# Hybrid decoder layer with a PEER expert stage: one weight half kept on chip, one projection half moved, twelve row buffers in place of six

## The chip, the cores and the metric
The kernel runs on 1 core of a Trainium2 chip. The metric is the device time in microseconds (us) of one execution; lower is better. A core has TensorE (PE, matmul; its weight loads are listed as PEld), VectorE (DVE), ScalarE (ACT), GpSimd (POOL) and SyncE (SP), and 16 DMA engines that serve all of its queues. Here SP issues the loads of weights (queue q1 in the profile) and POOL issues gathers of expert rows (queue q0).

## The reference
One layer on x (256 tokens x 1024, float32), with a memory of 256 tokens:
- RMSNorm, one projection `h @ w_in` to 3072 + 8 columns, 8 MoBA heads of 64 with a relative bias, 8 forgetting-attention heads of 64, an RMSNorm of either half, then `x += o @ w_out` (1024 x 1024).
- Cross-attention to the memory, 4 heads of 256, with `w_xq`, `w_xk`, `w_xv`, `w_xo` (1024 x 1024 each): `x += ...`.
- PEER: `h = RMSNorm(x)`, a routing query `h @ w_peer_query` (1024 x 1024, 8 heads of 2 x 64), scores against 2 x 128 sub-keys per head, the best 16 of either side, the best 16 of their 256 sums, and for each token and head 16 experts out of 16384:

```
u  = expert_down[eidx];  a = gelu(einsum('cd,chkd->chk', xc, u))
vv = expert_up[eidx];    y = einsum('chk,chkd->cd', g * a, vv)
```

`g` is the softmax of the 16 top scores. So each token reads 8 x 16 = 128 rows of `expert_down` and as many of `expert_up`. The output is a final RMSNorm. All in float32.

## The kernel before
**Tiles.** The 256 tokens are two tiles (t = 0, 1) of 128 tokens, one token per partition. `expert_down` and `expert_up` lie side by side in one table, so a gather of one slot brings 128 rows of 2048 floats, 1.05 MB: the first half of a row is for the dot product, the second is what is summed up. There are 2 x 128 slots n = 0 to 255 (`SPT` = 128 in a tile).

**Steps of a slot n.** POOL issues the gather into a row buffer (L554). DVE takes the dot product of the row's first half with the token (`dot`, L1017). ACT computes gelu, multiplies by the gate and writes a diagonal matrix of the result (`weight`, L722, L726, L729). PE multiplies that diagonal with the row's second half and accumulates (`up`, L1311: two products of 512 columns, which the profile lists as 4 MATMULs) and then increments `up_used`. There are `NS` = 6 row buffers: gather n waits until `up_used` says that slot n - 6 is done. Four of them are in `QKVB`, two in `SPARE`. `dots`, `gelu`, `wgt` and `diag` have 6 places as well.

**Order of the work.** Every engine runs a list of steps, written out by hand, in order (`main`, L120 to L176). It holds everything of tile 0 up to its routing query and all of tile 1's self-attention. Then come the slots. What tile 1 still needs (cross-attention, its routing query, its scores) and the second half of tile 0's routing query is put between tile 0's slots by the list `slots` (L179 to L189): PE does a step right after `up` of the slot named there, a step with four numbers in four quarters, and ACT and DVE do their part of it 4 slots later (`LAG`). The choice of experts for head H + 1 is spread over the slots of head H on DVE (`TOP`).

**Steps that the change touches.** `wout(t, i)` is output half i (512 columns) of `o @ w_out` of tile t, 8 products of 512 columns on PE; `wq(t, i)` is half i of the routing query, four heads, each 8 products of 128 columns; `sc` are the scores; `xq`, `xS`, `xPT`, `xO`, `xo` are cross-attention. In front of the slots the order is: a quarter of `wout(1, 1)`, the first routing head (`wq_first`) and its `top` (the choice of experts of head 0), the other three quarters of `wout(1, 1)`, `wq(0, 0)`, `sc(0, 0)`, `sc(0, 1)`, all of `wout(1, 0)`, then slot 0.

**Weights.** Weight halves of 2.1 MB are loaded by SP, in a fixed order, into six slots of the tile `weights` (`SLOT`, L73); `load_block` (L460) first waits until the last product that reads what lay there has been done (`used_up`). `w_peer_query`'s first half is loaded twice: early into `SPARE` for tile 0 (`wq_early`, L516), and again into weight slot 0, where `w_out`'s first half lay, for tile 1. Its second half goes into weight slot 1, where `w_out`'s second half lay, and serves both tiles. So SP's order here is: wait for `wout(1, 1)`, load half 1; wait for `wout(1, 0)`, load half 0; wait for `xo(1, 0)`, load the final gain. Since `SPARE` holds `wq_early`, gather 4 waits for `wq(0, 0)` (L551).

Of the kernel before, what the change touches and what calls it, by code (L numbers as in the profile page):

```python
# [60 lines left out]
def hybrid_layer(nc, A, out, bias_scratch):  # L61
# [96 lines left out]
    for part in range(4):  # L158
# [15 lines left out]
    main += rest[1][:1] + [("square_p", 0, 0), ("pT", 0, 1), ("start", 0, 0), ("wq_first", 0, 0), ("y_start", 0, 0),  # L174
                           ("sc_first", 0, 0), ("sc_first", 0, 1), ("root_p", 0, 0), ("top", 0, 0), ("y_start", 0, 1)]
    main += rest[1][1:] + [("wq", 0, 0), ("sc", 0, 0), ("sc", 0, 1)] + rest[0]  # L176


    slots = [((0, 1, 3, 4), ("wq", 0, 1)), (8, ("sc", 0, 2)), (9, ("sc", 0, 3)),  # L179
             (11, ("xT", 1, 0)), (11, ("xT", 1, 1)), (13, ("root_x", 1, 0)), (16, ("rstd_x", 1, 0)),  # L180
             ((19, 21, 23, 25), ("xq", 1, 0)), ((27, 29, 31, 33), ("xq", 1, 1))]
    for h in range(XH_N):
        slots += [(37 + 5 * h, ("xS", 1, h)), (42 + 5 * h, ("xnorm", 1, h)), (44 + 5 * h, ("xPT", 1, h)),
                  (49 + 5 * h, ("xO", 1, h))]
    slots += [((69, 71, 73, 75), ("xo", 1, 0)), ((77, 79, 81, 83), ("xo", 1, 1)), (85, ("xg", 1, 0)),
              (88, ("xg", 1, 1)), (89, ("square_p", 1, 0)), (90, ("pT", 1, 0)), (90, ("pT", 1, 1)),
              (91, ("root_p", 1, 0)), (95, ("rstd_p", 1, 0)), ((97, 99, 101, 103), ("wq", 1, 0)),
# [52 lines left out]
    with ctx:  # L240
# [156 lines left out]
        row_in = [sem(f"row_in{i}") for i in range(NS)]  # L397
# [55 lines left out]
        def _(sp):  # L453
# [64 lines left out]
            for b in (1, 0):  # L518
                load_block("w_peer_query", b)
# [40 lines left out]
        def _(act):  # L560
# [157 lines left out]
            def weight(n):  # L718
# [9 lines left out]
                act.wait_ge(w_done, n + 1)  # L728
                nc.scalar.activation(diag[:, i, :], ident[:, :], ACT.Copy, scale=wgt[:, i:i + 1])\  # L729
# [21 lines left out]
        def _(dve):  # L751
# [302 lines left out]
        def _(pe):  # L1054
# [67 lines left out]
            def step(name, t, i, part=None):  # L1122
# [183 lines left out]
            def up(n):  # L1306
# [56 lines left out]
```

## Time and profile before

| | us |
|---|---|
| timed, median of 3 (lowest, highest) | 937.75 (935.33, 939.22) |
| the profiled execution | 927.9 |
| its span, first to last instruction | 926.1 |
| PE / PEld / DVE / ACT / POOL busy | 815.2 / 457.9 / 556.4 / 443.6 / 242.6 |

The mean granted TensorE clock was 0.985 of full speed. The profiled execution is 1% below the timed ones; durations below are all from it. In a timeline each line begins with the start in us and the time in us from first to last of the merged instructions; "xN" is how many; brackets hold idle time ahead of it and what ended that.

### The profile page before, as it was taken

What the parts mean: (1) busy time and instruction counts of PE and PEld (TensorE: products, weight loads), DVE (VectorE), ACT (ScalarE), POOL (GpSimd) and SP (SyncE); (2) the same over time, 40 slices, a digit from 0 to 9 for tenths busy, and PEclk for the clock granted to TensorE, in tenths of its full rate; (3) what the DMA queues carried; (4) which work ended last, traced back from release to release, by engine and by line L of the source; (5) the groups of instructions that cost most, each with busy time, mean ns of one, the idle gap of its engine ahead of it and who ended that gap; (6) DMA issues with size and microseconds to landing.
All of it is one profiled execution on the core that took longest, in us unless ns stands there. A gap on an engine that the chain in (4) does not pass through costs nothing.

```text
span 926.1 us, 9462 instructions
## 1 busy us (share of the span) xinstructions
PE 815.2 (88%) x3195; PEld 457.9 (49%) x3195; DVE 556.4 (60%) x1345; ACT 443.6 (48%) x1088; POOL 242.6 (26%) x267
## 2 busy tenths in 40 slices
PE   7999999999989899888898999977877788787875
PEld 7999986687555365343343455432322222232322
DVE  5555333213456776777767758776766766676543
ACT  5435564324134645664546545464453545445343
POOL 0000000000023333334334333433333333333430
PEclk9999999999999999999999999999999999999999
DMA  9896632061099999999999999999999999999995
GB/s 334 227 312 244 205 115 91 1 230 44 1 371 413 415 422 419 413 416 421 419 409 421 421 413 417 418 410 416 421 422 421 422 421 416 421 408 423 409 422 218
DMA packets 64339, 316.33 MB, mean 342 GB/s; under 512 B 7907, under 2 KB 12068, under 8 KB 31524
## 3 DMA queue, kind: packets, MB, share of 16 engines
q0 software_dynamic: 36864, 268.45, 70.1%
q1 hardware_dynamic: 26348, 45.70, 13.9%
q10 hardware_dynamic: 1080, 1.59, 1.1%
q8 instruction: 25, 0.41, 0.2%
q14 instruction: 22, 0.18, 0.1%
HBM read 313.10 MB, written 2.62 MB: 341 GB/s over the span
## 4 chain that ended last, share of the span: by engine, by line
PE 53%; DMA 29%; ACT 10%; DVE 6%; issue 2%; POOL 0%; SPq 0%; POOLq 0%
DMA qkvb<-in_expert_rows,expert_idx 22%; PE y L1311 14%; PE v_bank L1311 8%; DMA spare<-in_expert_rows,expert_idx 6%; PE h_psum L1087 5%; PE v_bank L1077 5%; PE a_bank L1077 4%; PE a_bank L1087 4%; PE v_bank L1087 3%; DVE qkvb L1017 3%; PE h_psum L1077 3%; ACT L722 2%; PE v_bank L1176 2%; ACT diag L729 2%; PE y L1197 1%
## 5 line engine op out<-in xcount | busy, mean ns | idle before, releaser
L554 POOL DMA_INDIRECT qkvb<-in_expert_rows,expert_idx x172 | 162.1, 942 | 530.3 <-DVE expert_idx L1000 256.8
L722 ACT ACTIVATE gelu<-dots,stat 128x1 f32<-128x1 f32 x256 | 75.1, 293 | 309.3 <-DVE dots L1017 308.7
L1311 PE MATMUL v_bank<-qkvb,diag 128*128 128x512 f32 x344 | 171.8, 630 | 45.5 <-ACT diag L729 45.5
L1311 PE MATMUL y<-qkvb,diag 128*128 128x512 f32 x344 | 161.8, 607 | 21.2 <-ACT diag L729 21.2
L1017 DVE CUSTOM_DVE_ANT_0 qkvb<-a_bank,qkvb 128x1024 f32<-128x1024 f32 x86 | 105.3, 1224 | 74.1 <-DMA qkvb<-in_expert_rows,expert_idx 74.1
L1017 DVE CUSTOM_DVE_ANT_0 qkvb<-h_psum,qkvb 128x1024 f32<-128x1024 f32 x86 | 105.1, 1223 | 60.3 <-DMA qkvb<-in_expert_rows,expert_idx 60.3
L1311 PEld LDWEIGHTS v_bank<-qkvb,diag 128*128 128x128 f32 x344 | 61.4, 194 | 155.4 <-ACT diag L729 105.1
L554 POOL DMA_INDIRECT spare<-in_expert_rows,expert_idx x84 | 79.0, 941 | 132.5 <-PE y L1311 65.9
L1311 PEld LDWEIGHTS y<-qkvb,diag 128*128 128x128 f32 x344 | 62.1, 191 | 100.6 <-issue 56.5
L729 ACT ACTIVATE diag<-ident,wgt 128x128 f32<-128x128 f32 x256 | 102.7, 401 | 8.3
L1311 PE MATMUL v_bank<-spare,diag 128*128 128x512 f32 x168 | 85.1, 635 | 20.5 <-ACT diag L729 20.5
L1311 PE MATMUL y<-spare,diag 128*128 128x512 f32 x168 | 78.0, 600 | 6.5 <-ACT diag L729 6.5
L726 ACT ACTIVATE wgt<-gelu,gates 128x1 f32<-128x1 f32 x256 | 75.4, 295 | 8.3
L1017 DVE CUSTOM_DVE_ANT_0 spare<-a_bank,spare 128x1024 f32<-128x1024 f32 x42 | 51.4, 1224 | 34.6 <-DMA spare<-in_expert_rows,expert_idx 34.6
L1311 PEld LDWEIGHTS v_bank<-spare,diag 128*128 128x128 f32 x168 | 30.3, 196 | 74.3 <-ACT diag L729 49.0
L1017 DVE CUSTOM_DVE_ANT_0 spare<-h_psum,spare 128x1024 f32<-128x1024 f32 x42 | 51.3, 1221 | 25.8 <-DMA spare<-in_expert_rows,expert_idx 25.8
L824 DVE TENSOR_TENSOR weights_r<-weights,spare_r 128x2048 fp32r<-128x2048 f32 x19 | 43.5, 2290 | 29.1 <-ACT spare_r L630 29.1
L1311 PEld LDWEIGHTS y<-spare,diag 128*128 128x128 f32 x168 | 30.2, 190 | 44.6 <-issue 28.9
L1077 PEld LDWEIGHTS a_bank<-x_and_h,weights 128*128 128x128 f32 x320 | 39.5, 195 | 11.2 <-issue 11.2
L630 ACT CAST spare_r<-weights 128x2048 fp32r<-128x2048 f32 x19 | 36.1, 1898 | 16.8 <-PE v_bank L1087 14.6
L1077 PE MATMUL a_bank<-x_and_h,weights 128*128 128x128 f32 x320 | 39.6, 278 | 0.8 <-ACT weights L709 0.8
L1087 PE MATMUL h_psum<-weights_r 128*128 128x256 f32 x128 | 36.2, 283 | 0.0
(204 smaller groups left out, 1142.8 us busy)
## 6 DMA issues: line engine op xcount, KB each, us to landing
weights<-in_w_in SPq DMA_DIRECT2D x5, 2048.0 KB, 33.2
weights<-in_w_xk SPq DMA_DIRECT2D x2, 2048.0 KB, 17.4
weights<-in_w_xv SPq DMA_DIRECT2D x2, 2048.0 KB, 10.7
weights<-in_w_out SPq DMA_DIRECT2D x2, 2048.0 KB, 8.9
weights<-in_w_xq SPq DMA_DIRECT2D x2, 2048.0 KB, 8.5
weights<-in_w_xo SPq DMA_DIRECT2D x2, 2048.0 KB, 12.1
weights<-in_w_peer_query SPq DMA_DIRECT2D x2, 2048.0 KB, 16.5
qkvb<-in_expert_rows,expert_idx POOLq DMA_INDIRECT x172, 9.9
```

The lines of the kernel that those rows point to most:

```text
L554: pool.indirect_dma_start(ROWS[n % NS], None, expert_rows, bass.IndirectOffsetOnAxis(ap=IDX[:, H % 3, k:k + 1], axis=0))\
L630: act.copy(WH_r[t % 2], half_block(t, W)).then_inc(high_ready, 1)
L722: nc.scalar.activation(gel[:, i:i + 1], dots[:, i:i + 1], ACT.Gelu, scale=rms("root_p", n // SPT)).then_inc(gelu_done, 1)
L726: nc.scalar.activation(wgt[:, i:i + 1], gel[:, i:i + 1], ACT.Copy, scale=GATE[:, H % 3, k:k + 1])\
L729: nc.scalar.activation(diag[:, i, :], ident[:, :], ACT.Copy, scale=wgt[:, i:i + 1])\
L824: nc.vector.tensor_tensor(half_block(t, W_r), half_block(t, W), WH_r[t % 2].bitcast(f32), ALU.subtract).then_inc(low_ready, 1)
L1017: nc.vector.tensor_tensor_reduce(out=ROWS[i][:, 0:D], in0=HP[n // SPT][:, :], in1=ROWS[i][:, 0:D], scale=1.0, scalar=0.0, op0=ALU.mult, op ...
L1077: ins = nc.tensor.matmul(bank[:, lo:lo + n], lhs(k), rhs(k), start=(k == 0), stop=(k == chunks - 1))
L1087: ins = nc.tensor.matmul(bank[:, lo:lo + n], a(k), b(k), start=(k == 0 and p == 0), stop=(k == KC - 1 and p == 2))
L1176: ins = nc.tensor.matmul(bank[:, 0:nk], Q[lo:lo + HD, t, c, :], K[lo:lo + HD, 0:t + 1, c, :], start=True, stop=i < NH)
L1197: ins = nc.tensor.matmul(y[:, i * HD:(i + 1) * HD], PT[:, n % 2, j * P:(j + 1) * P], V[:, j, i * HD:(i + 1) * HD], start=(j == 0), stop=(j ...
L1311: ins = nc.tensor.matmul(YP[t][:, b * BLK:(b + 1) * BLK], diag[:, i, :], ROWS[i][:, D + b * BLK:D + (b + 1) * BLK], start=False, stop=n % ...
```

## The change
- `SLOT` and the load order no longer have a second load of `w_peer_query`'s first half. `wq_early` stays in `SPARE` and serves tile 1 too.
- In front of the slots, `wout(1, 0)` takes the places that `wout(1, 1)` had; `wout(1, 1)` is done in quarters after slots 2, 4, 6, 8.
- `wq(0, 1)` moves from slots 0, 1, 3, 4 to 11, 13, 15, 17, its scores from 8, 9 to 22, 23; `xT` from 11 to 13, `xq` from 19 to 33 to 24 to 38; the other steps of cross-attention by 2 to 4 slots; `wq(1, ...)` and later stay.
- 12 row buffers: the 4 in `QKVB`, 2 where `w_out`'s first half lay (free from `wout(1, 0)` on), 2 in the second halves of `w_xq`'s slots (from `xq(1, 1)`, slot 38), 2 in `mem_k` and `mem_v` (from `xO(1, 3)`, slot 68), and 2 in `SPARE` (from `wq(1, 0)`, slot 103). A planner gives each gather the buffer that is free soonest, so there are 6 until slot 38, then 8, 10, 12.
- `dots`, `gelu`, `wgt`, `diag` still have 6 places; `dot` now waits for the gelu, and the diagonal for the `up`, of slot n - 6.

```diff
-        blocks += [(name, b) for b in range(cols)]
+        blocks += [(name, b) for b in range(cols) if (name, b) != ("w_peer_query", 0)]
-    SLOT = dict(zip(blocks, (0, 1, 2, 3, 4, 0, 1, 2, 3, 4, 0, 1, 2, 3, 4, MEM_SLOT, 0, 1)))
+    SLOT = dict(zip(blocks, (0, 1, 2, 3, 4, 0, 1, 2, 3, 4, 0, 1, 2, 3, 4, MEM_SLOT, 1)))
...
-    main += rest[1][:1] + [("square_p", 0, 0), ("pT", 0, 1), ("start", 0, 0), ("wq_first", 0, 0), ("y_start", 0, 0),
+    main += rest[0][:1] + [("square_p", 0, 0), ("pT", 0, 1), ("start", 0, 0), ("wq_first", 0, 0), ("y_start", 0, 0),
                            ("sc_first", 0, 0), ("sc_first", 0, 1), ("root_p", 0, 0), ("top", 0, 0), ("y_start", 0, 1)]
-    main += rest[1][1:] + [("wq", 0, 0), ("sc", 0, 0), ("sc", 0, 1)] + rest[0]
-    slots = [((0, 1, 3, 4), ("wq", 0, 1)), (8, ("sc", 0, 2)), (9, ("sc", 0, 3)),
-             (11, ("xT", 1, 0)), (11, ("xT", 1, 1)), (13, ("root_x", 1, 0)), (16, ("rstd_x", 1, 0)),
-             ((19, 21, 23, 25), ("xq", 1, 0)), ((27, 29, 31, 33), ("xq", 1, 1))]
+    main += rest[0][1:] + [("wq", 0, 0), ("sc", 0, 0), ("sc", 0, 1)]
+    slots = [((2, 4, 6, 8), ("wout", 1, 1)), ((11, 13, 15, 17), ("wq", 0, 1)), (13, ("xT", 1, 0)), (13, ("xT", 1, 1)),
+             (14, ("root_x", 1, 0)), (18, ("rstd_x", 1, 0)), (22, ("sc", 0, 2)), (23, ("sc", 0, 3)),
+             ((24, 26, 28, 30), ("xq", 1, 0)), ((32, 34, 36, 38), ("xq", 1, 1))]
...
+        ROWS = [QKVB[:, 2 * i:2 * i + 2, :].rearrange("p a x -> p (a x)") for i in range(NB)]
+        ROWS += [W[:, wslot("w_out", 0), 2 * D * i:2 * D * (i + 1)] for i in range(2)]
+        ROWS += [W[:, wslot("w_xq", b), 2 * D:4 * D] for b in range(2)]
+        ROWS += [KM[:, :, :].rearrange("p c x -> p (c x)"), VM[:, :, :].rearrange("p a x -> p (a x)")]
+        ROWS += [SPARE[:, 2 * i:2 * i + 2, :].rearrange("p a x -> p (a x)") for i in range(2)]
+        last_of = dict(zip(range(NS, len(ROWS)), [st for st in (("xq", 1, 1), ("xO", 1, XH_N - 1), ("wq", 1, 0))
+                                                  for _ in range(2)]))
+        leaves = {st: at[-1] if isinstance(at, tuple) else at for at, st in slots}
+        free_from = {i: leaves[st] for i, st in last_of.items()}
+        BUF, USE, TAKES_FROM = [], [], []
+        for n in range(T * SPT):
+            before = {i: max([m for m in range(n) if BUF[m] == i], default=None) for i in range(len(ROWS))}
+            at = {i: before[i] if before[i] is not None else free_from.get(i, i - NS) for i in range(len(ROWS))}
+            i = min(at, key=lambda i: (at[i], i))
+            BUF.append(i); USE.append(BUF.count(i)); TAKES_FROM.append(before[i])
...
-            for b in (1, 0):
-                load_block("w_peer_query", b)
+            load_block("w_peer_query", 1)
...
                 if n == NB:
-                    pool.wait_ge(a_full, AN[("wq", 0, 0)] + 1)
-                if n >= NS:
-                    pool.wait_ge(up_used, n - NS + 1)
+                    pool.wait_ge(*full(("wout", 1, 0)))
+                if TAKES_FROM[n] is not None:
+                    pool.wait_ge(up_used, TAKES_FROM[n] + 1)
+                elif BUF[n] in last_of:
+                    pool.wait_ge(*full(last_of[BUF[n]]))
...
+                if n >= NS:
+                    act.wait_ge(up_used, n - NS + 1)
                 nc.scalar.activation(diag[:, i, :], ident[:, :], ACT.Copy, scale=wgt[:, i:i + 1])\
...
-                    early = t == 0 and i == 0
-                    w, bank = wq_early if early else wblk("w_peer_query", i), ab[AN[key] % 2]
+                    w, bank = wq_early if i == 0 else wblk("w_peer_query", i), ab[AN[key] % 2]
```

## Rows read from the trace of the kernel before
**Rows 1.** The page's slices: DMA busy tenths, and GB/s moved, in 40 slices.
```profile
DMA  9896632061099999999999999999999999999995
GB/s 334 227 312 244 205 115 91 1 230 44 1 371 413 415 422 419 413 416 421 419 409 421 421 413 417 418 410 416 421 422 421 422 421 416 421 408 423 409 422 218
```
**Rows 2.** Line L554, the gathers: what POOL waited for (us, times), and landing.
```profile
  PE y L1311: 208.4, 126
DMA to landing us min/median/max: 6.5/9.9/15.1
```
**Rows 3.** Timeline of one late slot, every engine.
```profile
908.28 1.23 DVE L1017 CUSTOM_DVE_ANT_0 qkvb<-a_bank,qkvb 128x1024 f32<-128x1024 f32 x1 [1.24 <-DMA qkvb<-in_expert_rows,expert_idx]
...
910.66 1.98 PE L1311 MATMUL v_bank<-qkvb,diag 128*128 128x512 f32 x4 [0.49 <-ACT diag L729]
910.77 1.22 DVE L1017 CUSTOM_DVE_ANT_0 qkvb<-a_bank,qkvb 128x1024 f32<-128x1024 f32 x1 [1.26 <-DMA qkvb<-in_expert_rows,expert_idx]
```
**Rows 4.** Stretches: busy us of engines, then granted clock, DMA share, GB/s.
```profile
255.00:260.00 5.00, 5.00 (x44) 4.78 (x43) 4.61 (x16) 0.49 (x2) 0.80 (x1) 1.00 0.68 224
270.00:275.00 5.00, 2.36 (x4) 1.14 (x5) 4.96 (x15) 2.97 (x9) 0.00 (x0) 0.84 1.02 420
275.00:280.00 5.00, 5.00 (x25) 3.53 (x25) 4.36 (x17) 1.98 (x6) 0.94 (x1) 0.82 1.00 395
270.00:330.00 60.00, 53.10 (x196) 29.40 (x197) 45.00 (x125) 33.99 (x85) 19.93 (x21) 0.97 1.02 415
385.00:600.00 215.00, 196.56 (x597) 94.63 (x597) 154.51 (x399) 114.12 (x301) 80.74 (x86) 1.00 1.01 416
600.00:910.00 310.00, 246.37 (x495) 88.53 (x493) 203.74 (x497) 146.08 (x403) 114.61 (x122) 0.97 1.01 418
660.00:770.00 110.00, 85.78 (x176) 29.83 (x174) 75.20 (x198) 51.45 (x141) 42.11 (x45) 1.00 1.01 421
```
**Rows 5.** Timeline where the slots begin.
```profile
255.41 14.62 SPq L465 DMA_DIRECT2D weights<-in_w_peer_query  x2
...
259.20 1.09 POOL L554 DMA_INDIRECT qkvb<-in_expert_rows,expert_idx  x1 [256.76 <-DVE expert_idx L1000]
...
262.50 7.13 PE L1077 MATMUL v_bank<-weights,x_and_h 128*128 128x512 f32 x16
...
272.64 3.10 PE L1311 MATMUL y<-qkvb,diag 128*128 128x512 f32 x4 [3.01 <-ACT diag L729]
```
**Rows 6.** The load issued at 255.4 us, size and us to landing; then the one at 269.7.
```profile
weights<-in_w_peer_query SPq DMA_DIRECT2D x1, 2048.0 KB, 7.8
weights<-in_w_peer_query SPq DMA_DIRECT2D x1, 2048.0 KB, 25.1
```
**Rows 7.** Queues from 273 to 278 us (packets, MB, share), then from 279 to 280.
```profile
q0 software_dynamic: 214, 1.62, 78.7%
q1 hardware_dynamic: 202, 0.41, 21.7%
...
q1 hardware_dynamic: 180, 0.37, 99.1%
```
**Rows 8.** PE timeline: pairs of slots with a quarter of `xo` (512 columns), then of `xq`.
```profile
451.39 1.88 PE L1077 MATMUL v_bank<-weights,scaled_gffn 128*128 128x512 f32 x4
453.11 3.60 PE L1311 MATMUL y<-spare,diag 128*128 128x512 f32 x8
456.54 1.88 PE L1077 MATMUL v_bank<-weights,scaled_gffn 128*128 128x512 f32 x4
...
334.88 1.95 PE L1077 MATMUL a_bank<-x_and_h,weights 128*128 128x128 f32 x16
336.67 3.60 PE L1311 MATMUL y<-qkvb,diag 128*128 128x512 f32 x8
```
**Rows 9.** A late gather of POOL, and the stretch behind it.
```profile
384.81 0.94 POOL L554 DMA_INDIRECT qkvb<-in_expert_rows,expert_idx  x1 [4.44 <-PE y L1311]
...
390.00:395.00 5.00, 4.21 (x11) 1.68 (x10) 3.69 (x9) 4.77 (x11) 2.45 (x3) 1.00 0.98 359
```

More of the change, by code:

```diff
@@ L173, in hybrid_layer @@
     main += [("xo", 0, 0), ("oT", 1, 0), ("xg", 0, 0), ("oT", 1, 1), ("xo", 0, 1), ("xg", 0, 1), ("pT", 0, 0)]
[L174 removed]
+    main += rest[0][:1] + [("square_p", 0, 0), ("pT", 0, 1), ("start", 0, 0), ("wq_first", 0, 0), ("y_start", 0, 0),
                            ("sc_first", 0, 0), ("sc_first", 0, 1), ("root_p", 0, 0), ("top", 0, 0), ("y_start", 0, 1)]
[L176 to L181 removed]
+    main += rest[0][1:] + [("wq", 0, 0), ("sc", 0, 0), ("sc", 0, 1)]
+    slots = [((2, 4, 6, 8), ("wout", 1, 1)), ((11, 13, 15, 17), ("wq", 0, 1)), (13, ("xT", 1, 0)), (13, ("xT", 1, 1)),
+             (14, ("root_x", 1, 0)), (18, ("rstd_x", 1, 0)), (22, ("sc", 0, 2)), (23, ("sc", 0, 3)),
+             ((24, 26, 28, 30), ("xq", 1, 0)), ((32, 34, 36, 38), ("xq", 1, 1))]
     for h in range(XH_N):
[L183 to L187, printed above, removed]
+        slots += [(41 + 5 * h, ("xS", 1, h)), (46 + 5 * h, ("xnorm", 1, h)), (48 + 5 * h, ("xPT", 1, h)),
+                  (53 + 5 * h, ("xO", 1, h))]
+    slots += [((72, 74, 76, 78), ("xo", 1, 0)), ((80, 82, 84, 86), ("xo", 1, 1)), (88, ("xg", 1, 0)),
+              (90, ("xg", 1, 1)), (91, ("square_p", 1, 0)), (92, ("pT", 1, 0)), (92, ("pT", 1, 1)),
+              (93, ("root_p", 1, 0)), (96, ("rstd_p", 1, 0)), ((97, 99, 101, 103), ("wq", 1, 0)),
               (108, ("sc", 1, 0)), (109, ("sc", 1, 1)), ((111, 113, 115, 117), ("wq", 1, 1)),
@@ L396, in hybrid_layer @@
         top_in, top_exp, idx_ready, gate_ready = sem("top_in"), sem("top_e"), sem("idx_ready"), sem("gate_ready")
-        row_in = [sem(f"row_in{i}") for i in range(NS)]
+        row_in = [sem(f"row_in{i}") for i in range(NB + 8)]
         dot_done, gelu_done, diag_done, up_used = (sem("dot_done"), sem("gelu_done"), sem("diag_done"),
@@ L435, in col @@
                     "root_p": 9 + 2 * t, "root_y": 12 + t}[name]
+        ROWS = [QKVB[:, 2 * i:2 * i + 2, :].rearrange("p a x -> p (a x)") for i in range(NB)]
[12 more added lines that the diff above has]
+            i = min(at, key=lambda i: (at[i], i))
+            BUF.append(i)
+            USE.append(BUF.count(i))
+            TAKES_FROM.append(before[i])
         def rms(name, t):
@@ L1015, in dot @@
                 i = n % NS
-                dve.wait_ge(row_in[i], 16 * (n // NS + 1))
-                nc.vector.tensor_tensor_reduce(out=ROWS[i][:, 0:D], in0=HP[n // SPT][:, :], in1=ROWS[i][:, 0:D],
+                rows = ROWS[BUF[n]][:, 0:D]
+                dve.wait_ge(row_in[BUF[n]], 16 * USE[n])
+                if n >= NS:
+                    dve.wait_ge(gelu_done, n - NS + 1)
+                nc.vector.tensor_tensor_reduce(out=rows, in0=HP[n // SPT][:, :], in1=rows,
                                                scale=1.0, scalar=0.0, op0=ALU.mult, op1=ALU.add,
@@ L1311, in up @@
                     ins = nc.tensor.matmul(YP[t][:, b * BLK:(b + 1) * BLK], diag[:, i, :],
-                                           ROWS[i][:, D + b * BLK:D + (b + 1) * BLK], start=False,
+                                           ROWS[BUF[n]][:, D + b * BLK:D + (b + 1) * BLK], start=False,
                                            stop=n % SPT == SPT - 1)
```

8 lines of the change are left out of this document (3 added, 5 removed).

## The prediction
> **What bounds the kernel now.** Read the slices first [rows 1]: from slice 12 on (about 260 us) the DMA engines are full to the end, at 408 to 423 GB/s. PE is busy for 88% of the span, but these slots do not wait for it: the stretches [rows 4] show PE at 78% from 660 to 770 us while DMA still moves 421 GB/s. The late slot [rows 3] confirms it: DVE waits for a row to land, and rows come 2.49 us apart (908.28 to 910.77). That is 268.4 MB / 256 = 1.049 MB a gather at 421 GB/s. So the slots are bound by bytes, and the rest of the span counts as the time ahead of the first gather (259.2 us, [rows 5]) and a tail behind the last landing that the change leaves alone. What can cost time is bytes, and any hole in the stream.
>
> Holes come from the ring. POOL waits for PE's `up` before every gather [rows 2], and a gather takes 9.9 us to land, 6.5 at least. From the landing of a row to the end of its `up` it is 910.66 + 1.98 - 908.28 = 4.36 us [rows 3]. With 6 buffers a turn is 6 x 2.49 = 14.9 us, so about 14.9 - 4.4 - 4.4 (a gather alone: 2.5 of transfer and some 1.9 of start and end, my estimate from the 6.5 at least) = 6 us is what PE may be late before the stream dries up.
>
> **Part 1, the load that goes.** 2.1 MB at 0.421 MB/us is 5.0 us. But it isn't all gained. In the kernel before, the first of the two loads starts at 255.4 us, before any gather, and 1.12 MB have moved by 260 [rows 4, 5]: that is time in which nothing else could run. In the kernel after, the load that stays waits for `wout(1, 1)`, now after slot 8, and moves wholly inside the full stream. Before, from 260 us: 268.44 + 4.19 + 0.52 (final gain) - 1.12 = 272.03 MB, at 421 GB/s 646.2 us, to 906.2. After: first row bytes about 260.9 (estimate: 1.7 us behind the issue at 259.2), 271.06 MB, 643.8 us, to 904.7. **Gain 1.5 us**, not 5.
>
> **Part 2, `wout(1, 0)` ahead, `wout(1, 1)` in the slots.** The 7.13 us that PE spends on a whole `wout` half right ahead of slot 0 [rows 5] go, and `up(0)` comes at about 266.5 instead of 272.6: row 0 lands at about 264 and its diagonal takes 2.37 us. Nothing is gained at the end, since DMA has work all that time; it restores the ring's slack. In the slots a pair of `up`s takes 456.54 - 453.11 = 3.43 us, 1.72 each, a `wout` quarter 1.72, a `wq` or `xq` quarter 1.79 [rows 8]. A pair with a quarter is 5.2 us against 4.97 of DMA: 0.2 late per pair, covered by the 6 us. DVE's addition of `wout(1, 1)` at slot 12 (0.7 us) lies in its idle time.
>
> **Part 3, the load and its reader.** Here I see the cost. Row n lands at about 264 + 2.49 n. With 4.36 us to the end of `up`, and the quarters after slots 2, 4, 6, 8, `up(8)` ends at about 288.8 and the last quarter at 290.5; SP then issues the load. PE reaches `wq(0, 1)` after `up(11)`, at about 295.7, and waits for all of it. Alone such a load took 7.8 us; issued into a queue full of gathers it took 25.1 [rows 6]. The queues say why: while both had work, q1 moved 202 packets and q0 214, one for one, but q1's are 2 KB and q0's 8 KB: 0.41 MB in 5 us, a fifth of the rate; only when q0 had run dry did q1 get all [rows 7]. At a fifth, 2.1 MB need 25 us; so the gathers are served first, and the load is the last to finish. PE waits, no `up` frees a buffer, and POOL stops at gather 17 (11 + 6). DMA is through with 18 gathers and the load, 20.97 MB, at 260.9 + 49.8 = 310.7. Then it has nothing: landing (1.0, estimate), the `wq` quarter 1.79, `up(12)` 1.72, 0.3 to POOL, 1.7 to the first bytes, **6.5 us of hole**. PE then has quarters and `xT` at slots 13, 15, 17 with a nearly dry ring, two rows per 5.2 to 6.1 us against 4.97: 1.5 more. After 3.0 us of idle the clock was 0.84 and 0.82 in two 5-us windows around 275 [rows 4, 5], which cost about 1.7 us (0.34 x 5); after some 15 us idle I take the same 1.7. **Sum 9.7.** Bounds: nothing (the load lands in time) and 12 (as before, with 3.4 for the clock and 2 more for a load that ends unevenly over the 16 engines). I take 9.7 because the order follows from the one-for-one row, and it would hold if SP issued the load 5 us sooner. DVE's and ACT's queues behind PE (dots up to 17, `xT` at 17) only wait with it.
>
> **Part 4, more buffers.** They act from slot 38 on, about 365 us, too late for part 3. What can they give? A late `up` lets POOL idle 4.44 us, and the stream falls to 359 GB/s behind it, 0.7 us lost [rows 9]. From 385 to 600 us the mean is 416, from 600 to 910 it is 418 [rows 4]; against 421: 215 x 5/421 + 310 x 3/421 = 2.6 + 2.2 = 4.8 us. With 8 to 12 buffers PE may be 11 to 20 us late. **Gain 4.5**, bounds 0 (the dips aren't the ring's) and 6 (against the best slices, 422 to 423). The stretch from 270 to 330 lost 60 x 6/421 = 0.9 us, which part 3 replaces: **gain 0.9**. The new waits of `dot` and the diagonal ask for slots 6 back, which are done: nothing. The planner issues the same 256 gathers, 0.94 us each.
>
> **Sum.** -1.5 + 9.7 - 4.5 - 0.9 = **+2.8 us**: span 928.9, profiled time 927.9 + 2.8 = 930.7. The timed median stands 9.85 us above the profiled time; the difference carried over gives 940.6.
>
> **Rivals.**
> A, the load lands in time. Were q1 served in larger turns, it would have its 2.1 MB by about 303, with two or three gathers still queued; PE goes on at 303, `up(12)` at 307, no hole. Then -1.5 - 4.5 - 0.9 and about 1 for PE's lateness: -5.9, **931.9**. For it: the first load's 7.8 us. Against: that one had no gathers beside it. The Trainium skill (DMA: Bandwidth & Descriptors, "Queues, rings and completion order") says that an engine changes queues only at packet boundaries, a packet being typically some 9 to 17 descriptors; if the load's 2 KB pieces travelled so and rows singly, the load would get well over half and this rival would hold. The trace's one-for-one count, with 2 KB against 8 KB, speaks against it.
>
> B, slower: the ring gives nothing back. If the stream's 416 to 418 GB/s is the memory's doing and only the dip of rows 9 is the ring's (0.7 us), the hole of part 3 stands almost unpaid: -1.5 + 9.7 - 0.9 - 0.7 = +6.6, and with the upper bound of the hole +8.9: **944.4 to 946.7**. It decides from a hole of about 7.8 us. For it: 4.1 of the 4.8 us lie spread thin over 525 us. Against: the stretch from 660 to 770 us, without such late gathers, holds 421 [rows 4].
>
> C, the timed runs lose more in holes than the profiled one. They are 10 us slower for a reason that no row gives. If half of that is late `up`s, 8 to 12 buffers win it back: 2.8 - 5 - some: **934**. Nothing in the trace speaks for or against.
>
> **How the numbers follow.** A measurement tells about 0.5% (4.7 us) from no change. Forecast 0.50, A 0.25, B 0.15, C 0.10. The forecast's own spread is about 4 us, so it is mostly "same", some "slower"; A straddles the bound with most beyond; B is slower, C mostly within or just under. Faster 0.30, same 0.41, slower 0.29. Range 931 to 947: A's price below, B's upper end above.
>
> **What would show it.** In the profile after: a PE idle of some 15 us behind `up(11)`, ended by the DMA of `w_peer_query`, with the load 20 us or more to landing; a window near 312 to 318 with almost no bytes; POOL's longest wait there. First gather at 259 us and `up(0)` near 266.5. From 385 us on 420 GB/s or more with no window under 400. Total moved 2.1 MB less. Wrong would be: a load landing within some 12 us, no empty window, or rates from 385 us still at 416 to 418.

## The result and the profile after

The kernel after takes **948.34 us** (median of 4 runs, 943.71 to 949.64) against 936.54 us of the kernel before in the same runs (927.60 to 939.22): a ratio of 1.0149 [1.0113, 1.0185], some 14 us slower (the two medians are 11.8 us apart). The forecast was 940.6 us with 931 to 947: the sign of its sum was right, the time lies above the range.

The profiled execution took 948.47 us, its span is 946.7 us, the mean clock 0.970. The page's slices of 23.7 us, against [rows 1]:

```profile
DMA  9897532070089599999999999999999999999992
GB/s 330 222 316 248 179 111 89 1 265 2 1 343 418 223 389 350 402 422 422 421 421 421 422 421 421 421 422 421 422 421 421 422 421 421 421 423 422 420 422 120
DMA packets 63303, 314.27 MB, mean 332 GB/s; under 512 B 7891, under 2 KB 12052, under 8 KB 30484
```

Three things are to be seen: a hole in slice 14 (223 GB/s, 308 to 331 us), a second, shallow one in slice 16 (350 GB/s, 355 to 379 us), and behind them 420 to 423 GB/s in every slice but the last.

The same in stretches of the kernel after (busy us and instructions of PE, PEld, DVE, ACT and POOL, then clock, DMA share, GB/s), against [rows 4]:

```profile
270.00:275.00 5.00, 4.73 (x6) 1.86 (x7) 2.33 (x3) 1.20 (x4) 0.68 (x1) 0.50 1.01 424
...
305.00:310.00 5.00, 0.00 (x0) 0.00 (x0) 3.23 (x7) 3.60 (x7) 0.00 (x0) 0.66 1.01 410
310.00:315.00 5.00, 0.00 (x0) 0.00 (x0) 1.82 (x5) 3.27 (x8) 0.00 (x0) 0.50 1.00 392
315.00:320.00 5.00, 3.13 (x14) 3.13 (x15) 1.05 (x2) 0.99 (x3) 0.00 (x0) 0.50 0.05 20
320.00:325.00 5.00, 5.00 (x23) 3.09 (x22) 0.00 (x0) 0.00 (x0) 1.69 (x2) 0.97 0.17 36
325.00:345.00 20.00, 19.66 (x81) 11.42 (x81) 11.16 (x27) 8.48 (x20) 7.55 (x9) 1.00 0.95 354
...
355.00:385.00 30.00, 30.00 (x138) 20.00 (x139) 16.84 (x45) 13.92 (x36) 9.39 (x10) 0.95 0.95 352
385.00:600.00 215.00, 198.87 (x616) 99.33 (x615) 155.25 (x402) 119.64 (x307) 83.18 (x88) 0.98 1.01 421
600.00:910.00 310.00, 246.70 (x511) 89.96 (x510) 208.35 (x518) 146.35 (x401) 118.37 (x126) 0.98 1.01 421
...
933.00:936.00 3.00, 2.21 (x5) 0.68 (x4) 1.23 (x2) 1.49 (x5) 0.00 (x0) 1.00 0.06 25
```

From 315 to 325 us the stream lost 10 - 5 x (20 + 36) / 421 = 9.3 us, from 325 to 345 us 20 x (421 - 354) / 421 = 3.2 us, from 355 to 385 us 30 x 69 / 421 = 4.9 us. In the kernel before, 300 to 345 us and 345 to 390 us both ran at 419 GB/s. From 385 us on 421 GB/s stand where [rows 4] had 416 and 418. The last line belongs to the end: three microseconds with a DMA share of 0.06, about what one busy engine of sixteen makes (16 x 0.06 = 1.0; the trace does not name the engines).

PE's timeline of the kernel after shows who made the two holes (start, us, in brackets the idle time and what ended it):

```profile
270.27 8.26 PE L1333 MATMUL y<-qkvb,diag 128*128 128x512 f32 x12 [4.66 <-ACT diag L749]
...
295.06 1.88 PE L1100 MATMUL v_bank<-weights,x_and_h 128*128 128x512 f32 x4
...
298.50 3.60 PE L1333 MATMUL y<-weights,diag 128*128 128x512 f32 x8
316.87 3.67 PE L1100 MATMUL a_bank<-x_and_h,weights 128*128 128x128 f32 x16 [14.78 <-DMA weights<-in_w_peer_query]
...
350.29 1.98 PE L1333 MATMUL y<-qkvb,diag 128*128 128x512 f32 x4
354.75 3.50 PE L1100 MATMUL a_bank<-x_and_h,weights 128*128 128x128 f32 x16 [2.48 <-ACT x_and_h L727]
```

The first line is the begin of slot 0: `up(0)` starts at 270.3 us, and the first three `up`s take 8.26 us at a clock of 0.50; it takes nothing from the stream, which runs at 424 GB/s meanwhile. The first hole is the predicted one: the last quarter of `wout(1, 1)` ends at 296.9 us, `up(11)` at 302.1, and then PE waits 14.78 us for the load. The quarter behind it takes 3.67 us where [rows 8] had 1.95, at a clock of 0.50. The second was not predicted: after `up(24)` PE waits 2.48 us for ACT to empty a bank of `a_bank`. POOL, in its timeline, stands behind both:

```profile
302.40 0.94 POOL L572 DMA_INDIRECT weights<-in_expert_rows,expert_idx  x1 [0.30 <-PE y L1333]
322.53 0.94 POOL L572 DMA_INDIRECT qkvb<-in_expert_rows,expert_idx  x1 [19.19 <-PE y L1333]
...
360.24 0.94 POOL L572 DMA_INDIRECT qkvb<-in_expert_rows,expert_idx  x1 [6.76 <-PE y L1333]
```

ACT's timeline of the same stretch tells why the bank came late:

```profile
353.73 0.40 ACT L749 ACTIVATE diag<-ident,wgt 128x128 f32<-128x128 f32 x1
354.04 0.57 ACT L727 COPY x_and_h<-a_bank 128x512 f32<-128x512 f32 x1
```

`sc(0, 2)` is done by PE after slot 22, but ACT's part of it (the copy) comes 4 slots later in its list, behind the diagonal of slot 26. `xq(1, 0)` starts after slot 24 and needs that bank. So PE, at slot 24, waits for a row two slots further on.

The load in the list of DMA issues, and the queues from 305 to 310 us, against [rows 6] and [rows 7]:

```profile
weights<-in_w_peer_query SPq DMA_DIRECT2D x1, 2048.0 KB, 19.9
```
```profile
q0 software_dynamic: 223, 1.59, 77.3%
q1 hardware_dynamic: 225, 0.46, 24.1%
```

19.9 us to landing, and again one piece for one piece: 225 of 2 KB against 223, most of them of 8 KB.

### The profile page after: what moved, and what is told of

The parts are those of the page before. It is cut to its first block, busy times and chain, and to the rows that moved or that the text cites. A ratio compares the mean times of both kernels' runs of the same rounds, so it can differ in the third digit from the quotient of the medians.

```text
span 946.7 us, 9962 instructions
## 1 busy us (share of the span) xinstructions
PE 821.4 (87%) x3195; PEld 463.3 (49%) x3195; DVE 557.6 (59%) x1345; ACT 446.4 (47%) x1090; POOL 242.7 (26%) x267
## 4 chain that ended last, share of the span: by engine, by line
DMA 46%; PE 40%; ACT 5%; issue 4%; DVE 4%; POOL 1%; SPq 0%; DVEq 0%
DMA mem_k<-in_expert_rows,expert_idx 28%; DMA qkvb<-in_expert_rows,expert_idx 10%; PE y L1333 10%; PE h_psum L1110 5%; PE a_bank L1110 4%; PE a_bank L1100 3%; PE h_psum L1100 3%; PE v_bank L1110 3%; PE v_bank L1100 3%; PE v_bank L1333 3%; DMA mem_v<-in_expert_rows,expert_idx 3%; DMA weights<-in_w_peer_query 2%; DMA weights<-in_expert_rows,expert_idx 2%; PE v_bank L1199 2%; PE y L1220 1%
## 5 line engine op out<-in xcount | busy, mean ns | idle before, releaser
L572 POOL DMA_INDIRECT qkvb<-in_expert_rows,expert_idx x108 | 101.9, 944 | 453.7 <-DVE expert_idx L1020 285.1
L1333 PE MATMUL y<-qkvb,diag 128*128 128x512 f32 x256 | 122.7, 614 | 15.3 <-ACT diag L749 15.3
L572 POOL DMA_INDIRECT weights<-in_expert_rows,expert_idx x92 | 86.6, 942 | 132.0 <-PE y L1333 69.2
L1333 PE MATMUL v_bank<-qkvb,diag 128*128 128x512 f32 x176 | 87.4, 624 | 23.6 <-ACT diag L749 23.1
L1333 PE MATMUL v_bank<-weights,diag 128*128 128x512 f32 x168 | 85.4, 639 | 21.5 <-ACT diag L749 21.0
L1333 PE MATMUL y<-weights,diag 128*128 128x512 f32 x200 | 94.5, 604 | 5.6 <-ACT diag L749 5.5
L1040 DVE CUSTOM_DVE_ANT_0 weights<-h_psum,weights 128x1024 f32<-128x1024 f32 x50 | 61.2, 1224 | 34.3 <-DMA weights<-in_expert_rows,expert_idx 33.2
L1040 DVE CUSTOM_DVE_ANT_0 qkvb<-a_bank,qkvb 128x1024 f32<-128x1024 f32 x44 | 53.9, 1224 | 38.9 <-DMA qkvb<-in_expert_rows,expert_idx 36.3
L1040 DVE CUSTOM_DVE_ANT_0 weights<-a_bank,weights 128x1024 f32<-128x1024 f32 x42 | 51.4, 1225 | 34.7 <-DMA weights<-in_expert_rows,expert_idx 31.4
L1100 PE MATMUL a_bank<-x_and_h,weights 128*128 128x128 f32 x256 | 34.5, 293 | 18.0 <-DMA weights<-in_w_peer_query 14.8
L1333 PE MATMUL v_bank<-spare,diag 128*128 128x512 f32 x80 | 38.8, 612 | 7.4 <-ACT diag L749 7.4
## 6 DMA issues: line engine op xcount, KB each, us to landing
weights<-in_w_xk SPq DMA_DIRECT2D x2, 2048.0 KB, 17.2
```

The costliest lines, as they stand in the source:

```text
L572: pool.indirect_dma_start(ROWS[BUF[n]], None, expert_rows, bass.IndirectOffsetOnAxis(ap=IDX[:, H % 3, k:k + 1], axis=0))\
L1040: nc.vector.tensor_tensor_reduce(out=rows, in0=HP[n // SPT][:, :], in1=rows, scale=1.0, scalar=0.0, op0=ALU.mult, op1=ALU.add, accum_out=d ...
L1100: ins = nc.tensor.matmul(bank[:, lo:lo + n], lhs(k), rhs(k), start=(k == 0), stop=(k == chunks - 1))
```

## The experiments

Ratios are to the kernel before in the same runs, with 95% intervals; 1% is 9.4 us. "Lost stream" is what the windows of 5 us lack against 421 GB/s, in us. The experiments ran beside the kernel before, the kernel after did not run again: what an edit to it removes is a difference of two ratios from different sessions, each known to some 0.3%.

### e1: both halves of `wout` of tile 1 ahead of the slots

```diff
-    main += rest[0][1:] + [("wq", 0, 0), ("sc", 0, 0), ("sc", 0, 1)]
+    main += rest[0][1:] + [("wq", 0, 0), ("sc", 0, 0), ("sc", 0, 1)] + rest[1]
-    slots = [((2, 4, 6, 8), ("wout", 1, 1)), ((11, 13, 15, 17), ("wq", 0, 1)), ...
+    slots = [((11, 13, 15, 17), ("wq", 0, 1)), ...
```


> The changed kernel, with wout(1, 1) put back ahead of the slots, behind wout(1, 0). SP then issues the load of w_peer_query's second half at about 273 us, some 11 slots ahead of its reader. Theory L (the load shares the DMA engines one piece for one with the gathers and is read only 3 slots after its issue): the load still takes 20 to 25 us to land, but PE does not wait at slot 11; the empty stretch of 9.4 us goes, with it the 3 us behind it. The wait of xq for the copy of the scores at slot 24 stays. Ratio to before 0.997 to 1.003, 12 us below the changed kernel. Rival P (PE has too much work in tile 0's slots: 7 us of wout more): gains the same, so this run alone does not tell them apart. Rival S (the changed kernel merely began its slots 3 us later, at a lower clock): ratio stays at 1.01 or more.

Measured: 936.18 us, **1.0019** [0.9987, 1.0051]. The load is now issued at 271.2 us, 34 us ahead of its reader, takes 25.0 us to landing and keeps nobody waiting; that refutes rival S. It removes 1.0149 - 1.0019 = 1.3%, **12 us**, with some 4.5 us of uncertainty either way. The other hole stands and is longer (345 to 390 us: 7.1 us lost). The waits and the stretch in e1:

```profile
342.99 3.75 PE L1100 MATMUL a_bank<-x_and_h,weights 128*128 128x128 f32 x16 [3.49 <-ACT x_and_h L727]
```
```profile
345.00:390.00 45.00, 45.00 (x192) 27.95 (x191) 27.32 (x68) 19.23 (x52) 17.07 (x19) 0.96 0.92 355
```

### e2: `xq` three slots later

```diff
-             ((24, 26, 28, 30), ("xq", 1, 0)), ((32, 34, 36, 38), ("xq", 1, 1))]
+             ((27, 29, 31, 33), ("xq", 1, 0)), ((34, 36, 38, 40), ("xq", 1, 1))]
```


> The changed kernel, only xq(1, 0) moved from slots 24, 26, 28, 30 to 27, 29, 31, 33 and xq(1, 1) from 32 to 38 to 34 to 40. In the changed kernel PE at slot 24 needs a PSUM bank that ACT empties only behind its slot 26. Theory B (that wait, its 2.5 us and the fallen clock after it, cost the 5 us of lost stream from 355 to 385 us): 3 to 5 us faster than the changed kernel, ratio to before about 1.010, no PE wait on the copy of the scores, stream above 400 GB/s from 350 us on. Rival P (xq's quarters, 5.2 us for two slots against 4.97, drain a ring that the hole at slot 11 has left nearly empty): no gain, the loss moves with xq.

Measured: 941.45 us, **1.0111** [1.0084, 1.0137]: 0.4%, **3.6 us** less than the kernel after. Alone that difference is within its uncertainty of 4 us; e1 against e3 and e9 shows the same edit once more, with 3.0 us, and the traces agree in its direction. The wait for the load stands as it was, that for ACT is gone, and 345 to 390 us is full: the loss did not move with `xq`, as rival P had it. PE's timeline and the stretch in e2:

```profile
312.67 3.78 PE L1100 MATMUL a_bank<-x_and_h,weights 128*128 128x128 f32 x16 [14.79 <-DMA weights<-in_w_peer_query]
```
```profile
345.00:390.00 45.00, 43.59 (x189) 26.10 (x189) 30.66 (x77) 21.43 (x59) 16.25 (x17) 1.00 1.01 418
```

### e3 and e9: both edits together, run twice

The edit is that of e1 and that of e2.

> Both of the edits: wout(1, 1) ahead of the slots, xq three slots later. Theories L and B together: nothing is left of the changed kernel's losses, the larger ring keeps its 4.5 us, the removed load its part: ratio to before 0.990 to 0.996, the DMA stream at 420 GB/s from the first gather to the last. Rival P gives the same within 1 us as the run with only wout ahead. Rival S: ratio above 1.0.

> The run with both edits and 12 buffers once more, so that the order of the two wout halves and the number of buffers stand crossed on one chip (four kernels). Here: wout(1, 0) first, 12 buffers. Accounting by bytes: 3 us slower than the swapped order, since its load moves wholly inside the stream. By the first two chips: 0.999.

Measured: 931.58 us, **0.9991** [0.9962, 1.0020], and 930.90 us, **0.9983** [0.9952, 1.0013]. No wait of PE for the load or for ACT's copy is left, and 265 to 390 us loses 3.1 and 2.9 us. The two causes together are worth 1.6%, 15 us, and account for the whole slowdown. But the expectation for e3 was 0.990 to 0.996, and what is left, all of the planned gain without its price, is -0.13%, **-1.2 us**; the prediction had -6.9 for it.

### e5: the load in 16 KB pieces

```diff
-            load_block("w_peer_query", 1)
+            sp.wait_ge(*used_up(*BEFORE[("w_peer_query", 1)]))
+            sp.dma_start(W[:, SLOT[("w_peer_query", 1)], :],
+                         A["w_peer_query"][0][0:BLK, :].rearrange("(p r) c -> p (r c)", p=P))\
+                .then_inc(w_full[SLOT[("w_peer_query", 1)]], 16)
```


> The changed kernel, with the same 2.1 MB load at the same place, but from a stretch of w_peer_query that is contiguous for each partition (16 KB), so the tile gets other weights than it should: pieces of up to 16 KB in place of 2 KB. Theory L with turns by piece: the load's share beside the gathers rises from a fifth to a half or more, it lands in 8 to 12 us in place of 20, PE waits 0 to 3 us at slot 11 in place of 14.8, and the kernel is 7 to 12 us faster than the changed one, ratio to before 1.003 or less. Rival Q (a load issued behind a full queue waits for the gathers issued earlier, whatever its pieces): still about 20 us to land, ratio 1.013 to 1.016. Rival P: no gain either, since wout stays in the slots.

Measured: 940.76 us, **1.0083** [1.0047, 1.0119], 6 us less than the kernel after; 7 to 12 were expected. The tile holds other weights than it should, so the experts of four heads are others. Same bytes, same place, but 12.0 us to landing in place of 19.9, and PE waits 6.88 us in place of 14.78. The queues from 298 to 303 us, and PE's timeline, in e5:

```profile
q1 hardware_dynamic: 92, 1.29, 61.0%
q0 software_dynamic: 112, 0.79, 38.0%
```
```profile
304.00 3.71 PE L1103 MATMUL a_bank<-x_and_h,weights 128*128 128x128 f32 x16 [6.88 <-DMA weights<-in_w_peer_query]
```

By count the queues still take turns, 92 against 112, but a turn of the load now carries 14 KB, so it has 61% of the bytes. The size of the pieces sets how long the load takes; that is the mechanism of part 3, and rival Q (the load waits for all gathers issued earlier) is refuted. Its wait is shortened, not gone: the gathers still have 38%.

### e4: only the ring, in the kernel before

The kernel before with the change's `ROWS`, `BUF`, `TAKES_FROM` and waits: 6 buffers, 8 from slot 33 on, 10 from slot 64 on. The core of the edit:

```diff
+        ROWS += [W[:, wslot("w_xq", b), 2 * D:4 * D] for b in range(2)]
+        ROWS += [KM[:, :, :].rearrange("p c x -> p (c x)"), VM[:, :, :].rearrange("p a x -> p (a x)")]
...
-                if n >= NS:
-                    pool.wait_ge(up_used, n - NS + 1)
+                if TAKES_FROM[n] is not None:
+                    pool.wait_ge(up_used, TAKES_FROM[n] + 1)
+                elif BUF[n] in last_of:
+                    pool.wait_ge(*full(last_of[BUF[n]]))
```


> The kernel before, with its order and both loads, and only the planner's row buffers: 6 until slot 33, 8 until 64, then 10. Theory D (the 16 DMA engines are not equally fast; more buffers let 15 of them run ahead, and the last one, which sets the end, gains nothing): the stream from 385 us on rises from 416 to 418 to 421 GB/s, but its end gets ragged, 5 us and more of under 100 GB/s behind it, and the time stays: ratio 0.998 to 1.002. Rival R (the prediction's part 4: the holes filled are time won): 4.5 us faster, ratio 0.994 to 0.996, a clean end.

Measured: 932.29 us, **0.9974** [0.9940, 1.0008]. 385 to 600 us and 600 to 900 us run at 421 GB/s, so the dips of [rows 4] are the ring's. But a gain of 4.5 us would be 0.9952, and it is -2.4 us with an interval that reaches zero. Its last 10 us before the last `dot` move 78 GB/s in the mean, where the kernel before moves 337.

### e6 and e10: e3 with 6 buffers, run twice

```diff
+        ROWS = ROWS[:NS]
```


> The changed kernel with wout(1, 1) ahead of the slots and xq three slots later, and only 6 row buffers to the end. Theory D: the same time as with 12 (ratio 0.997 to 1.002), a clean end, stream at 416 to 418 GB/s. Rival R: 4 to 5 us slower than with 12, ratio 1.003 or more.

> wout(1, 0) first, 6 buffers. Theory D (uneven engines give back what the buffers win): within 0.2% of the run with 12 buffers. Rival R (holes filled are time won): 0.5% slower.

Measured: 935.70 us, **1.0009** [0.9974, 1.0044], and 934.31 us, **1.0014** [0.9981, 1.0047]. This is the change without its two waits and without its buffers: +0.12%, +1.1 us, where part 1 and the 0.9 us of the stretch from 270 to 330 us were to give -2.4. The buffers are the difference to e3 and e9: 0.18% and 0.31%, **2.3 us**, between theory D's 0.2% or less and rival R's 0.5%. The traces say where the rest of their gain goes. First e3, then e10:

```profile
385.00:600.00 215.00, 197.55 (x607) 96.97 (x607) 154.84 (x403) 120.22 (x309) 86.33 (x93) 0.99 1.01 421
600.00:900.00 300.00, 238.72 (x478) 85.95 (x479) 200.61 (x493) 141.65 (x388) 110.06 (x118) 0.97 1.01 421
910.00:915.00 5.00, 4.00 (x10) 1.36 (x9) 2.52 (x5) 1.98 (x6) 0.00 (x0) 1.00 0.66 275
915.00:920.00 5.00, 4.04 (x10) 1.43 (x9) 2.53 (x5) 1.98 (x6) 0.00 (x0) 1.00 0.09 38
```
```profile
385.00:600.00 215.00, 196.39 (x597) 95.16 (x595) 155.02 (x399) 119.19 (x305) 80.95 (x86) 0.99 1.01 416
600.00:900.00 300.00, 236.65 (x476) 84.76 (x476) 198.54 (x491) 142.08 (x390) 110.88 (x118) 0.97 1.01 416
910.00:915.00 5.00, 3.97 (x8) 1.36 (x8) 2.46 (x4) 2.01 (x7) 0.00 (x0) 1.00 1.00 418
915.00:920.00 5.00, 3.97 (x8) 1.35 (x8) 2.47 (x4) 2.06 (x7) 0.00 (x0) 1.00 0.07 28
```

With 12 buffers the stream is 5 GB/s faster for 515 us, 6.1 us. At the end it frays: counted back from the last `dot` (921.5 us in e3, 917.8 us in e10), the windows of 1 us move 8, 25, 33, 25, 41, 49, 66, 123, 262 and 336 GB/s in e3, and 8, 25, 164 and 410 in e10. Against 421 that is 7.7 us and 2.6 us missing: 5.1 of the 6.1 us are given back.

The other profiles say the same. Lost stream from 390 to 900 us, and in the 10 us before the start of the last `dot`:

| row buffers at the end | profiles | 390 to 900 us | last 10 us |
|---|---|---|---|
| 6 | before, e6, e8, e10, e12, e13 | 4.6 to 9.2 | 2.0 to 2.9 |
| 10 or 12 | after, e1 to e5, e7, e9, e11, e14 | -0.3 to 0.5 | 7.1 to 8.1 |

With 6 buffers the first number differs between two profiles of one and the same kernel: 7.7 in e6, 5.8 in e10. The profile from which the forecast was made has the lowest of the six, 4.6.

### e7 and e11: e3 with `wout(1, 1)` first, run twice

```diff
-    main += rest[0][:1] + [("square_p", 0, 0), ("pT", 0, 1), ("start", 0, 0), ("wq_first", 0, 0), ("y_start", 0, 0),
+    main += rest[1][:1] + [("square_p", 0, 0), ("pT", 0, 1), ("start", 0, 0), ("wq_first", 0, 0), ("y_start", 0, 0),
...
-    main += rest[0][1:] + [("wq", 0, 0), ("sc", 0, 0), ("sc", 0, 1)] + rest[1]
+    main += rest[1][1:] + [("wq", 0, 0), ("sc", 0, 0), ("sc", 0, 1)] + rest[0]
```


> As the run with both edits and 12 buffers, but wout(1, 1) in front of wout(1, 0), so that SP issues the remaining load at about 255 us, ahead of the first gather, as the kernel before does. Gathers 4 and 5 then wait for wout(1, 0), about 270 us. Accounting by bytes: 1.1 MB of the load move before any gather, the stream has 2.1 MB less than before, 5.0 us: ratio 0.993 to 0.997 if no hole opens while PE catches up behind slot 0. Rival H (the second load of the kernel before filled holes of the start, from 273 to 290 us, and was free): the stream falls under 380 GB/s between 275 and 295 us, ratio 0.998 or more.

> wout(1, 1) first, 12 buffers. If the first measurement holds: ratio 0.989 to 0.994 to before, the fastest of the four.

Measured: 926.64 us, **0.9910** [0.9872, 0.9949], and 927.50 us, **0.9947** [0.9925, 0.9970], where 0.989 to 0.994 had been expected. It is the fastest version, ahead of both kernels. The load that stays starts at once when `wout(1, 1)` is done, ahead of the rows, and lands in 8.0 us. The hole that rival H expected is there, in e7:

```profile
270.00:295.00 25.00, 17.77 (x34) 7.26 (x35) 21.03 (x63) 12.85 (x34) 9.32 (x10) 0.90 0.97 377
```

But the time is that of the byte account (0.993 to 0.997) or better, not H's 0.998 or more.

### e8 and e12: e7 with 6 buffers, run twice

The edit is that of e6 on e7.

> The same with 6 row buffers to the end. Theory D: equal to the run with 12 within 0.2%. Rival R: 4 to 5 us slower than it.

> wout(1, 1) first, 6 buffers. Theory D: within 0.2% of the run with 12. Rival R, which the first pair in this order favours (0.8% apart): 4 to 8 us slower than with 12, ratio to before 0.997 to 1.000.

Measured: 931.26 us, **0.9993** [0.9963, 1.0023], and 934.40 us, **1.0017** [0.9987, 1.0048]. This is the kernel before with its order in front of the slots, without the second load, with `wq(0, 1)` and cross-attention later and two of its six buffers elsewhere: 1.0005 in the mean. With 6 buffers, taking the load out gains nothing, whichever half comes first. Here the buffers are worth 0.83% and 0.70%, three times as much as in e3 and e9; theory D had expected the two rings within 0.2%.

### e13 and e14: the kernel before, and e4, with the second load cut to an eighth

```diff
-            for b in (1, 0):
-                load_block("w_peer_query", b)
+            load_block("w_peer_query", 1)
+            sp.wait_ge(*used_up(*BEFORE[("w_peer_query", 0)]))
+            sp.dma_start(wblk("w_peer_query", 0)[:, 0:1, :],
+                         A["w_peer_query"][0].rearrange("(k p) c -> p k c", p=P)[:, 0:1, 0:BLK])\
+                .then_inc(w_full[SLOT[("w_peer_query", 0)]], 16)
```


> The kernel before, with its second load of w_peer_query (the first half again, issued at 270 us) cut to an eighth, 0.26 MB; the rest of that tile keeps old values, so tile 1's routing is not the reference's. Nothing else moves. Accounting by bytes (part 1): 1.84 MB less in the stream, 4.4 us faster, ratio 0.9953. Theory H (in the start of the slots, where up(0) comes at 272.6 us and POOL at 276 and 280, the load ran in holes): the holes open instead, 3 to 5 us of lost stream between 275 and 295 us, ratio 0.998 to 1.001.

> The same cut load with the planner's row buffers (10 from slot 64 on), everything else as before. If buffers and load are independent: the ratio of the small load times that of the buffers alone (0.9974), so 0.993 by bytes or 0.996 by theory H. The first gather to the last dot product is then 2 us below the run with the full load if the holes are filled at once, since more buffers come only from slot 33 on.

Measured: 933.67 us, **1.0022** [0.9991, 1.0052], and 931.35 us, **0.9991** [0.9964, 1.0018]. (Tile 1's experts are others than the reference's.) So 1.84 MB less in the stream, 4.4 us of it, and no gain: 0.9953 was expected by bytes for e13, 0.993 for e14, and 0.9991 is also above theory H's 0.996. Where they were, e13 has a hole:

```profile
270.00:295.00 25.00, 21.99 (x95) 13.61 (x95) 19.23 (x55) 11.55 (x30) 5.71 (x6) 0.93 0.95 359
280.00:285.00 5.00, 5.00 (x25) 3.30 (x24) 4.18 (x14) 1.98 (x6) 0.93 (x1) 1.00 0.79 279
```

The kernel before moves 414 GB/s from 270 to 295 us. Without the load the same stretch falls to 359: (414 - 359) x 25 / 421 = 3.3 us of the 4.4. PE comes late to the first slots (`wout(1, 0)` is ahead of them), no buffer is free, and only the load gave DMA something to do. [Rows 7] already showed it: at 279 us q1 had 99.1% for itself.

## Why the prediction was wrong

Three steps of the sum failed. It had no term for the wait of `xq(1, 0)` for ACT's copy (3.6 us measured). It priced the buffers at the stream's mean rate and had nothing for the stream's end, which gives back 5.1 us. And part 3 came out 2.3 us short. A further 3.5 us between forecast and timing, of part 1 and the 0.9 us beside it, are not explained.

**Part 3, the load and its reader: mechanism right, size under.** Predicted: PE idle behind `up(11)` ended by `w_peer_query`, an empty window near 312 to 318 us. Measured: that wait, 14.78 us, and 20 GB/s from 315 to 320 us. e1 removes it and 12 us with it (e3 and e9 against e2: 11.6 us); 9.7 were predicted, **2.3 us short**. The terms, from the trace: hole and clock 8.2 predicted, 9.3 measured; nearly dry ring behind it 1.5 predicted, 3.2 measured. The term for the clock was right though its reason was thin: it had been taken from an idle time of 3 us, and after 14.8 us at a granted clock of 0.50 the quarter took 3.67 us in place of 1.95, 1.7 us more. What was short is the end of the load, 1.0 us by an estimate that no row gave (332 GB/s from 314 to 315 us, 90 from 315 to 316, then 8, and PE goes on at 316.87), and the refilling of the ring. That q0 and q1 take turns by pieces, on which it all rested, is supported by e5, which gave the load larger pieces and left its bytes and its place alone.

The rule of the Trainium skill weighed there (DMA: Bandwidth & Descriptors, "Queues, rings and completion order": queues change at packet boundaries, a packet being some 9 to 17 descriptors) did not come out as a larger share for the load. The counts were 202 to 214, 225 to 223 and 92 to 112; what the load gains, it gains by larger pieces.

**A step that was missing: `xq(1, 0)` after slot 24.** The prediction counted the moved cross-attention steps as quarters of PE's time and did not ask which bank they take. Moving `sc(0, 2)` to slot 22, with ACT's part at slot 26, and `xq` to 24 put two slots of waiting into PE's list. e2 shows it: **3.6 us**.

**Part 4, the buffers: 4.5 predicted, 2.3 measured.** The rates from 385 us on came out as forecast, 421 for 416 to 418. The step that failed is that the sum runs the stream at its mean rate up to the last landing, and has no term for its end. The tail behind the last landing is indeed left alone (10.4 us from the start of the last `dot` to the end in both kernels); it is ahead of it that the deeper ring frays the stream: the last 10 us lack 7.8 us in the kernel after and 2.0 in the kernel before, and 5.1 us of e3's gain are given back. The 2.3 us hold for the order of the changed kernel; the same buffers are worth 2.4 us in e4, 2.9 in e14 against e13 and 7.2 in the swapped order.

**Part 1 and the 0.9 us of the stretch from 270 to 330: 2.4 predicted, none measured, and why stays open.** Without the load, without the two waits and with 6 buffers the time is +1.1 us in e6 and e10; with e8 and e12 the mean is 1.0008. e13 shows that in the kernel before the second load ran where little else could, and was nearly free. That does not refute the sum of part 1, though. In the changed kernel the load moved wholly inside a full stream, as it says (423 GB/s from 270 to 295 us), and most of its 1.5 us is in the profiles: in the kernel before, the first load still moves 1.21 MB behind the issue of the first gather and the first row bytes come 3.1 us behind it, in the kernel after 1.8. What the timings lose again is not found: the profiles of e6 and e10 lack 7.7 and 5.8 us from 390 to 900 us where that of the kernel before lacks 4.6, but e13, with the buffers of the kernel before, lacks 9.2.

**Part 2** was right: nothing gained, nothing lost. `up(0)` came at 270.3 us and not at 266.5, 3.0 us of it because the first gather came at 262.2 and not at 259.2, and the ring covered it.

**The sum.** +2.8 predicted; +2.3 for part 3, +3.6 for the bank, and 5.7 of gains that are not there (3.5 of part 1 and the 0.9 us, 2.2 of part 4): +14.4 us, against 14 measured. The terms come from pairs of ratios that are each known to some 0.3%, 3 us, so the agreement is luck in part. The two profiles give a sum of their own. From the first gather to the start of the last `dot` it is 656.5 us before and 674.0 after, +17.5. Lost stream up to 390 us is 18.3 us against 0.9 (+17.4, nearly all of it the load's hole and the bank's), from 390 to 900 us -0.1 against 4.6 (-4.7), in the last 10 us 7.8 against 2.0 (+5.8), and the first row comes 1.3 us sooner behind its issue: +17.2.

**The rivals.** A (the load lands in time) is refuted: 19.9 us and a hole. B had the right side, but not the mechanism: the ring's dips were its own. It named 946.7 at most, since it too lacked the bank. C (timed runs lose more in holes) is not borne out, though no run was made for it. The kernel before ran from 927 to 943 us on one chip, and its quick runs have a higher mean clock than its slow ones (0.986 in the run of 927.35 us, 0.973 in that of 942.61). e8 and e12 are one kernel; their profiles span 936.9 and 925.8 us, and the first gather comes at 269.8 and 258.5: the whole difference of 11 us lies ahead of the slots, where no ring is at work. First e8, then e12:

```profile
225.00:250.00 25.00, 24.50 (x88) 15.11 (x87) 8.59 (x24) 7.18 (x19) 0.00 (x0) 0.78 0.00 1
```
```profile
225.00:250.00 25.00, 24.49 (x96) 13.56 (x96) 9.31 (x22) 7.59 (x17) 0.00 (x0) 1.00 0.00 1
```

Why the clock falls there in one execution and not in another is open.

**What stays open.** In the timings `wout(1, 1)` first is worth 0.6% with 12 buffers (0.9929 against 0.9987 in the mean) and under 0.1% with 6 (1.0005 against 1.0012). The profiles do not show that it hangs on the buffers: from the first gather to the last `dot` e7 and e11 take 656.2 and 655.1 us, e3 and e9 658.2 and 658.3, and with 6 buffers e8 and e12 take 656.7 and 657.0, e6 and e10 661.9 and 658.3, so the swapped order is some 3 us ahead either way (e6 and e10, one kernel, are themselves 3.6 apart). Nor is it settled why e7 and e11 gain from the load that is gone and e14 does not. Up to 390 us e14 lacks 7.5 us of stream, e7 and e11 4.3 and 3.6; in these `wq(0, 1)` comes 11 to 13 slots later, and PE catches up sooner. No run moves that step alone. Which DMA engine trails at the end, and why, was not tried either.

## What to carry to other kernels

A load put just ahead of its reader, into a queue that is full of gathers, gets its share by pieces and not by bytes: price its landing by piece counts from the trace, and place its issue that far ahead. When a step moves in a hand-written list, look also for the buffer it takes over and for the instruction that empties it, with the lag of its engine. Bytes that run in a hole of the stream can be free, as the second load of the kernel before was (e13); look at what the other queue did at that moment before you count them. And a mean rate does not price the end of a stream: look at its last 10 us by themselves.

## What the runs showed of the hardware

- Two queues on the same DMA engines took turns nearly piece by piece, whatever the size: 202 to 214 and 225 to 223 with pieces of 2 KB against mostly 8 KB, 92 to 112 with pieces of 14 KB in the mean. The same 2.1 MB took 7.8 to 8.0 us with the engines to itself, 12.0 us with large pieces, and 19.9 to 25.1 us with small ones among gathers.
- With 10 or 12 row buffers the stream did not end at once: in e3 about 25 GB/s moved in the last 4 us ahead of the last `dot`, a DMA share of 0.06. With 6 (e10) it was 2 us. The mean rate was higher with the deep ring all the same (421 against 416).
- Over 14.8 us without a matmul the granted clock went to 0.66 and then 0.50, that is to 1.2 GHz, and stayed at 0.50 in the window in which PE began again; 3 us of idle had shown 0.84 and 0.82 in two windows [rows 4], and 4.66 us of idle ahead of slot 0 of the kernel after 0.91 and 0.50.
- The first gather came anywhere between 257.2 and 269.8 us in the profiles, in kernels that do nearly the same up to there, and 11.3 us apart in e8 and e12, which are one kernel: the span alone does not compare two slot orders; the stretch from the first gather to the last `dot` does better.
